# Clearing DRAM rows from another queue, and re-ordering the start of the first expert, in a one-core trunk kernel

## The reference, cut to what matters

```python
def recurrent_group(x_in, y_in, ...):
    xc = causal_conv(x_in, conv_w, conv_b)
    return rg_lru(xc, wa, ba, wx, bx, lam) * jax.nn.gelu(y_in)

def swiglu(x, wg, wu, wd):
    return (jax.nn.silu(x @ wg) * (x @ wu)) @ wd

def moe_ffn(x, router_w, wg, wu, wd):
    logits = (x @ router_w).astype(jnp.float32)
    top_val, top_idx = lax.top_k(logits, TOP_K)            # 2 of 8
    w = jax.nn.softmax(top_val, axis=-1)
    gate = jnp.sum(jax.nn.one_hot(top_idx, N_EXPERTS) * w[..., None], axis=-2)
    y = jnp.zeros_like(x)
    for e in range(N_EXPERTS):                             # d_ff of an expert: 1408
        y = y + gate[..., e:e + 1] * swiglu(x, wg[e], wu[e], wd[e])
    return y
```

## Time and profile before

| | |
|---|---|
| median of 3 runs | 1330.28 us (1328.93 to 1330.73) |
| the profiled execution's own time | 1324.21 us |
| its span | 1322.4 us |
| mean granted clock of TensorE | 0.989 |
| busy PE, DVE, ACT, POOL | 1267.1, 949.1, 677.8, 130.1 us |
| mean DMA rate over the span | 197 GB/s |

### The profile page before, as it was taken

One profiled execution on the slowest core, in us unless ns is written; L12 is line 12 of the kernel. 1 busy time (PEld: TensorE's weight loads), 2 busy tenths in 40 slices (PEclk: granted clock), 3 DMA queues, 4 the chain that ended last, 5 costly groups with the idle time before them and its releaser, 6 DMA issues.

```text
span 1322.4 us, 24758 instructions
## 1 busy us (share of the span) xinstructions
PE 1267.1 (96%) x10314; PEld 819.6 (62%) x10375; DVE 949.1 (72%) x1304; ACT 677.8 (51%) x993; POOL 130.1 (10%) x113
## 2 busy tenths in 40 slices
PE   7999999999999999999999999979999999999992
PEld 3457565444444444444457565569979988989981
DVE  7886885886531556334886885688788799989996
ACT  6256774443210333112265774365586687787772
POOL 0011320600000000031011000501200000000002
PEclk9999899999999999999999999999999999999997
DMA  8551881444310443012551000168999999999975
GB/s 272 184 151 35 317 334 60 146 186 149 118 67 0 150 165 148 0 33 103 194 150 35 20 1 21 61 238 325 360 381 376 349 348 398 374 352 398 359 307 208
DMA packets 43134, 260.26 MB, mean 197 GB/s; under 512 B 6522, under 2 KB 7546, under 8 KB 28554
## 3 DMA queue, kind: packets, MB, share of 16 engines
q1 hardware_dynamic: 33626, 224.77, 46.1%
q0 software_dynamic: 8960, 33.26, 7.0%
q10 hardware_dynamic: 432, 0.59, 0.1%
HBM read 218.00 MB, written 33.65 MB: 190 GB/s over the span
## 4 chain that ended last, share of the span: by engine, by line
PE 84%; issue 6%; DVE 4%; DMA 3%; POOL 1%; ACT 1%; SPq 0%; POOLq 0%; DVEq 0%; ACTq 0%
PE bank L1177 20%; PE bank L1178 20%; PE bank L1179 19%; PE bank L1387 5%; PE bank L1435 3%; PE bank L1405 3%; PE bank L727 1%; PE bank L726 1%; PE bank L725 1%; DMA expert_slots<-arena,row_index 1%; PE bank L735 1%; PE bank L737 1%; PE bank L736 1%; POOL expert_slots L2520 1%; PE bank L1242 1%
## 5 line engine op out<-in xcount | busy, mean ns | idle before, releaser
L988 DVE SCALAR_TENSOR_TENSOR arena<-arena 128x3072 f16<-128x3072 f32 x86 | 288.2, 3352 | 10.8 <-ACT arena L842 9.1
L842 ACT ACTIVATE arena<-arena 128x3072 f16<-128x3072 f32 x86 | 237.9, 2767 | 41.1 <-DMA arena<-in_ew 19.5
L1177 PE MATMUL bank<-arena 128*128 128x144 bf16 (+3 forms) x877 | 215.1, 264 | 6.0 <-DVE arena L988 2.7
L1178 PE MATMUL bank<-arena 128*128 128x144 f16 (+3 forms) x878 | 215.4, 264 | 0.1
L1179 PE MATMUL bank<-arena 128*128 128x144 bf16 (+3 forms) x867 | 211.2, 263 | 0.0
L1178 PE MATMUL bank<-hl,wring_hi 128*128 128x512 f16 x352 | 133.4, 379 | 1.5 <-issue 0.6
L1179 PE MATMUL bank<-hh,wring_lo 128*128 128x512 bf16 x341 | 129.2, 379 | 0.0
L1177 PE MATMUL bank<-hh,arena 128*128 128x512 bf16 x338 | 128.1, 379 | 1.0
L1178 PE MATMUL bank<-hl,arena 128*128 128x512 f16 x338 | 128.1, 379 | 0.0
L1177 PE MATMUL bank<-hh,wring_hi 128*128 128x512 bf16 (+1 forms) x333 | 126.3, 379 | 1.0 <-DVE wring_lo L1885 0.5
L1179 PE MATMUL bank<-hh,arena 128*128 128x512 bf16 x319 | 120.9, 379 | 0.0
(11 more groups left out here) (334 smaller groups left out, 2521.2 us busy)
## 6 DMA issues: line engine op xcount, KB each, us to landing
arena<-in_ew SPq DMA_DIRECT2D x86, 1536.0 KB, 9.1
arena<-in_dw SPq DMA_DIRECT2D x22, 1536.0 KB, 6.4
wstage<-in_w_chunk SPq DMA_DIRECT2D x44, 512.0 KB, 3.9
expert_results<-iota POOLq DMA_DIRECT2D x9, 2048.0 KB
arena<-in_cmp_w SPq DMA_DIRECT2D x2, 2048.0 KB, 8.0
arena<-arena SPq DMA_DIRECT2D x60, 64.0 KB, 2.1
expert_slots<-iota POOLq DMA_DIRECT2D x5, 512.0 KB
expert_results<-wstage SPq DMA_DIRECT2D x5, 512.0 KB
```

The lines of the kernel that those rows point to most:

```text
L842: act.activation(ew_hi_[:, G % EP, :], ew[:, G % ES, :], ACT.Copy, scale=SW).then_inc(M["hi_ready"], 1)
L988: dve.scalar_tensor_tensor(out=ew_lo_[:, G % EP, :], in0=ew[:, G % ES, :], scalar=SW, in1=ew_hi_[:, G % EP, :], op0=ALU.mult, op1=ALU.subt ...
L1177: pe.matmul(out, w_hi, x_hi, start=first, stop=False)
L1178: pe.matmul(out, w_hi, x_lo, start=False, stop=False)
```

## The change: what it does

1. **Clearing.** POOL no longer issues the zeros. The 19 transfers move to SP's queue (`clear_rows`), in layer 0, just ahead of weight chunk 18; SP waits only for the zeros of `iota`. `load_rows` and the scatters' semaphore no longer count them together.
2. **The GELU polynomial on POOL** ("gate products"), in both layers, waits for the extremes of attention step 3 as well.
3. **The first expert on PE:** `upper(0)` moves behind the last gather, to the head of `begin`.
4. **On ACT:** a one-element Silu is put ahead of everything in the experts, which loads its table there; the copies of the gathered tokens j = 4 to 7 now all come ahead of `first_hi(2)`, which stood between j = 5 and 6.
5. **On DVE:** `places` becomes a generator in four parts; one part runs after each of chunks G = 4, 5, 6 and 7. Part 3 holds the row numbers.

```diff
@@ begin (PE)
+                pe.wait_ge(M["gathered"], KC // 2)
+                pe.wait_ge(M["first_hi"], 1)
+                upper(0)
                 pe.wait_ge(M["first_hi"], 2)
                 upper(1)
@@ experts_pe
                 if j == KC // 2:
-                    pe.wait_ge(M["gathered"], KC // 2)
-                    pe.wait_ge(M["first_hi"], 1)
-                    upper(0)
                     pe.wait_ge(*ready("tok_l", TT - 1))
@@ experts_act
             act.sem_inc(M["y_out"], 4)
+            act.activation(small[:, 244:245], eps[:, 0:1], ACT.Silu)
             first_hi(0)
             for j in range(KC):
                 gathered(0, j, bank[GATHER_BANK[j % 4]], 0, CAPS[0])
-                if j in (3, 5):
-                    first_hi(j // 2)
-            for p in (3, 4):
+                if j == 3:
+                    first_hi(1)
+            for p in (2, 3, 4):
                 first_hi(p)
@@ experts_dve
+            place_parts = places()
...
-                if G == 2 * LEAD:
-                    places()
+                if G >= 2 * LEAD:
+                    next(place_parts, None)
@@ load_rows (SP)
-                sp.wait_ge(*ready("blank", "slotted"))
+                sp.wait_ge(*ready("slotted"))
@@ places (DVE): a yield after each of
                         by_rank(gate, lg)
+                        yield
...
                         link(dve.tensor_tensor(key_first, key_first, key_second, ALU.subtract))
+                        yield
...
                             dve.tensor_scalar(row_index[:, at:at + TT], which, -1.0, None,
                                               ALU.add).then_inc(*signal("rows"))
+                        yield
@@ gpsimd, for each layer and chunk c
+                    pool.wait_ge(*ready("nmx", l, 3, 0))
                     pool.wait_ge(*ready("feat", l, feat_index("y", c)))
                     pool.wait_ge(*ready("lru_step", "scan", l, c))
...
-                if l == 0:
-                    pool.wait_ge(*ready("nmx", l, 0, 0))
-                    (the transfers of clear_rows, issued by pool)
@@ sync
+            def clear_rows():
+                sp.wait_ge(*ready("by_pool", "zeros"))
+                blank = results_dram.rearrange("(p a) d -> p (a d)", p=P).rearrange("p (a n) -> p a n", n=256)
+                for a in range(0, blank.shape[1], 16):
+                    n = min(16, blank.shape[1] - a)
+                    sp.dma_start(blank[:, a:a + n, :], iota[:, 0:256].unsqueeze(1).broadcast_to([P, n, 256])
+                                 ).then_inc(*signal("blank", by=16))
+                for e in range(2, NE):
+                    (its rows, up to 128 at a time, likewise)
...
+                    if l == 0 and j == NF + WR + 1:
+                        clear_rows()
                     ...
                     chunk(J)
```

More of the change, by code:

```diff
@@ L2521, in _ @@
                         ap=row_index[:, at + i:at + i + 1], axis=0), tok_[:, i, :], None
-                        ).then_inc(*signal("blank", "slotted", by=16))
+                        ).then_inc(*signal("slotted", by=16))
             pool.wait_ge(M["all_stored"], 1)
@@ L2558, in swap_halves @@
                                      ).then_inc(*signal(f"swapped{n % 2}", l, n, by=16))
+            def clear_rows():
[6 more added lines that the diff above has]
+                for e in range(2, NE):
+                    rows = slots_dram[e * YROWS:e * YROWS + CAPS[e], :].rearrange("r (a n) -> r a n", n=256)
+                    for a in range(0, CAPS[e], P):
+                        w = min(CAPS[e] - a, P)
+                        sp.dma_start(rows[a:a + w], iota[0:w, 0:256].unsqueeze(1)
+                                     .broadcast_to([w, DM // 256, 256])).then_inc(*signal("blank", by=16))
             def spread_kpe(l):
```

## The result

| | before | after |
|---|---|---|
| median of 6 runs each, side by side | 1329.24 us (1327.84 to 1330.73) | 1336.81 us (1333.87 to 1339.01) |
| ratio after/before | | 1.0061, 95% interval 1.0044 to 1.0078 |
| the profiled execution's own time | 1324.21 us | 1339.01 us |
| its span and granted clock | 1322.4 us, 0.989 | 1337.2 us, 0.977 |

The change makes the kernel slower, by 7.6 us. I had said 1325.8, in a range up to 1333. The profiled execution before is faster than each of these six, and the one after is the slowest of its six, so they lie 14.8 us apart; I read stretches from them, not their total.

What follows compares the result with a forecast made beforehand. The prediction took PE, busy 96% of the span, to bound the kernel. Its terms -2.9 + 0 + 0 - 1.9 + 0 + 0.3 gave -4.5, from 1330.28 to 1325.8 us, range 1321.5 to 1333.

Steps and rivals of the forecast that it cites:

- step 2: Attention, both layers: delaying POOL's GELU polynomial swaps one DVE block for another, 0 a layer, bounds -1.1 and +2.9.
- rival C: Attention: POOL and DVE collide, PE gaps and half clock in both layers, +1.3 us in all; chance 7%.
- Step 1: Attention, layer 0: zeros issued from SP instead of POOL let it run as layer 1 does, -2.9 us.
- Step 3: First expert's start: table load leaves the line and token copies come earlier, -1.9 us, bounds -0.5 and -2.1.
- Step 4: Experts: four parts of `places` remove PE's 2.4 us, worth 0 at the end; later scatters give +0.3, bounds -1 and +8.7.
- Rival D: Experts: row numbers 8.7 us later make chunk 15 8.7 later, PE idles there, +3.9 in all, 1334.2; chance 12%.

Runs made afterwards that it cites:

- gelu_early: Changed kernel without POOL's wait for the extremes of attention step 3; median 1323.7 us, ratio 0.9971 to the kernel before.
- phase_places: places_early with the second chunk's three POOL operations in attention each starting with a DVE reduction; median 1320.4 us, ratio 0.9941 to the kernel before.
- late6: Changed kernel with POOL's wait for the extremes of attention step 6 in place of step 3; ratio 0.9982 to the kernel before.
- late_half: Changed kernel with POOL's six operations at their old place, repeated behind attention step 3 on 256 of 512 columns; ratio 1.0034 to the kernel before.
- clear_only: Kernel before with only the zeros moved to SP's queue; median 1326.3 us, ratio 0.9973 to the kernel before.
- first_undone: Changed kernel with the first expert's start (`upper(0)`, copies, table load) as before; 1338.4 us, ratio 1.0080 to the kernel before.
- early_first_old: places_early with the first expert's start (`upper(0)`, copies, table load) as before; 1320.7 us, ratio 0.9951 to the kernel before.
- late_small: Changed kernel with POOL's six operations at their old place, repeated behind attention step 3 on one column; median 1326.1 us, ratio 0.9990 to the kernel before.
- rows_later: gelu_early with the experts' first row load one weight chunk later in SP's list; 1324.5 us, ratio 0.9983 to the kernel before.
- places_early: gelu_early with the four parts of `places` behind chunks 2 to 5; ratio 0.9958 to the kernel before.

## Why the prediction was wrong

**The step that failed is 2, the GELU polynomial behind step 3, "0 a layer", bounds -1.1 and +2.9.** It costs 6.1 us in layer 0 and 5.9 in layer 1 (after against gelu_early), 12.0 where I had 0. The block that it removes was sized well: I had -1.1, and phase_places, which removes it and adds none, gains 0.9. The block that it adds was put at +1.1 and costs about 6.9 (85.1 to 85.3 against the 78.3 of phase_places). The mechanism was named, as rival C, and given 7%. Three things in its working were wrong:

- *The phase.* I let POOL's operations fall anywhere, half of them under reductions. But the added wait is for a reduction's signal, and what stands in DVE's list right behind it is a gate product and two scalings. POOL and DVE start the block together. late6 and phase_places show that phase and place decide: about the same block costs 0.6 at step 6 (78.9 against 78.3), and none is left when the second chunk's operations each start with a reduction.
- *The room.* "Soon after PE multiplies values, which gives DVE room": the first products of values come only after the second gap. Up to there PE's list is scores that wait for exponentials.
- *The price of half clock.* I bounded each layer by half of POOL's busy time, 2.9. PE's idle time grows by 2.36 - 0.90 = 1.5 (0.68 and 0.22 are the undisturbed layer's), and the rest, some 4.5, is matmuls at half clock: 0.9 on L1389, 0.9 on L1407, 0.9 on L1426, 1.7 on L1437. Rival C used the 2.9 of the earlier trace rows for it and let layer 0 merely keep its loss; layer 0 lost 3.2 more than before. Its point of decision, "about 1.3 us more idle PE", was near: late_half has 1.1 more and falls to half clock in one layer of two.

The port rule of the Trainium skill (SBUF - State Buffer, "SBUF: two separate sides") says which DVE operations take the lock that GpSimd also needs: those in a two-port mode or with two inputs in SBUF. The rows agree: L2247, L2240 and L1887 are held, reductions out of PSUM (1.22, 1.28) and the reciprocal (0.15) are not; that L2247, with one tensor as input, runs in a two-port mode no row shows. It was the right rule, and I used it to say that the collision moves, without asking where to.

**Step 1** was right: -2.9 on the clean layer, cost of SP nothing, and in clear_only the zeros are issued 41 us ahead of chunk 19 (186.1 and 227.1).

**Step 3** (-1.9): at chunk 2 it gives 0.9 to 1.1 between first_undone or early_first_old and their partners. Table load and copies moved as said. What blurs it is the clock in the lower gathers, which follow a gap on PE. In the changed kernel's profile the gap is 2.2 us and the clock in 885 to 890 us is 0.66, and ACT waits for them; in the kernel before the gap, there ahead of `upper(0)`, is 2.8 us and the clock stays at 1.00, so the two profiles differ by only 0.4 at chunk 2. The new order is not what brings half clock. Three of the four kernels with the old start have it as well, and late_small and rows_later, with the new start and the same gap of 2.2, have clock 1.00. Like against like, chunk 2 comes at 18.5 and 19.2 for 20.4 at full clock, and at 19.8 to 20.1 for 21.0 to 21.8 at half. That is 1.6 on the mean at full clock and 1.3 at half, where I had 1.9. By chunk 15 little of it is left, and at the end nothing is measured.

**Step 4** was right in kind: no waits near chunks 5 to 7, parts that fit (1.8, 1.7, 1.6 and 1.3 us), and a gain worth 0 at the end. Row numbers come 8.2 us later in the profile (59.5 against 51.3), and chunk 15 some 0.7 later on the mean of all kernels, where I had +0.3. The wait at chunk 15's product in the changed kernel, where I had said 3 to 4 us:

```profile
975.30 0.67 PE L738 MATMUL bank<-arena 128*112 128x512 f16 x1 [3.88 <-DVE arena L1022]
```

What I did not price is half clock behind it (0.67 for a product that takes 0.38 at full clock), which all eight kernels with parts from chunk 4 on have and no other. Rival D, the whole delay passing, didn't come.

**The sum** with the measured terms: -2.9 (step 1) + 12.0 (step 2) + about 0 (steps 3 and 4, not told from 0 by any run) = +9, against +7.6 of the medians and +8.1 of the ratio, the interval of which reaches from 5.8 to 10.4.

## What to carry to other kernels

When POOL work is moved behind a semaphore, look at what the signalling engine does next: the two start together, so here an operation on SBUF released by DVE's reduction met DVE's SBUF operations every time, not on average. Put such work under PSUM reductions, or where PE has work queued. And when a wait may open a gap of a microsecond or two on a PE that already idles at that place, price the matmuls of the next 10 us at half clock: the clock was three quarters of the loss here. A saving upstream of a transfer that is late anyway gave nothing that could be measured; moving what the transfer waits for (places_early) brought the load forward by 4.8 us.

## What the runs showed that was not expected

- The same two PE gaps (0.68 and 1.36 us) leave the clock at 1.00 in one layer and halve it in the other of one execution. A kernel near that edge has a spread of its own: late_half 1322.6 to 1338.2, where the twelve runs of gelu_early lie within 8.2 us. The first expert shows the same: with the new start and a gap of 2.2 us the clock falls to 0.50 in eight profiles and stays at 1.00 in two, late_small and rows_later, and it stays at 1.00 behind the 2.8 us of the kernel before.
- A gate product of 128x2 or 128x4, 0.16 us alone, lasts until POOL's operation beside it ends: 1.03, 1.27.
- SP's ten issues of up to 2 MB take 48.5 us, 4.8 each on the mean, and nothing but SP waits for them.
- The first expert's chunk 2 and the landing of the inputs at the start (PE's first wait was 4.9 to 7.5 us long) vary by 1.6 and 2.6 us between kernels with equal code there. Single profiles can't settle an edit of a microsecond there; attention, which repeats within 0.2, mostly can.
